# Expert rows gathered by index and expert results summed on chip by weighted selection products, in a three-block transformer kernel

## The chip, the core and the metric

The kernel runs on one NeuronCore of a Trainium2 chip. Its engines run side by side, each with its own instruction stream: TensorE (PE) multiplies matrices into PSUM, with a stream of its own for loading the stationary operand (PEld); VectorE (DVE), ScalarE (ACT) and GpSimd (POOL) work on rows in SBUF and PSUM; SyncE (SP) here only issues transfers. ACT and POOL issue transfers as well. Sixteen DMA engines carry them between HBM and SBUF. Engines wait for each other by semaphores. The metric is device time in microseconds, the median of several executions; everything is float32.

## What is computed

Three blocks act on 512 tokens of 1024 features: differential attention, latent attention (MLA), and a block of dilated attention beside a convolution, followed by a hierarchical mixture of experts. Each block scales and shifts its normed input by a modulation row, `silu(c) @ w + b`. The change touches the first modulation row and, above all, the mixture of experts:

```python
grp = argmax(hf @ w_rg + b_rg)                       # one of 4 groups
top_val, top_idx = lax.top_k(e_logits[grp], 2)       # two of its 8 experts
top_w = softmax(top_val) * p_grp
# every token goes to 2 of 32 experts; rows sorted by expert, padded
def expert_block(args):
    xblk, e = args
    return (silu(xblk @ w_gate[e]) * (xblk @ w_up[e])) @ w_down[e]
out = zeros((T + 1, D)).at[buf_tok].add(yb * buf_w[:, None])[:T]
y = x + gate * out ; result = rms_norm(y, g_final)
```

The three matrices of an expert are 1024x512, 1024x512 and 512x1024: 2 MB each, 6 MB an expert, 192 MB for all 32.

## The kernel before

**Expert stage.** `route` (on DVE) ranks the 32 experts by how many rows they have, and gives each rank a fixed number of row slots: 3 fixed experts with 64, 7 big ones with 128, 7 middle ones with 64, 15 small ones with 32 (`ROWS_OF`); rows beyond that would go to a loop of further items, which is skipped if none are left over. `Plan` makes 32 items in a fixed order: three fixed ones, then seven times (big, small, middle, small), then one small. An item has one or two pieces of at most 64 rows; there are 39 pieces (24 of 64 rows, 15 of 32).

**Rows in and out through HBM.** POOL writes zeros over the HBM buffer `expert_rows` (12.7 MB) and the end of `expert_results` early on (L1407), after routing scatters each of the 512 normed rows to its two slots (8 indirect transfers, L1423), and then loads each item's block of rows (`load_rows`, L1427). After an item ACT stores the gated results to `expert_results` (L1352). When all are stored, POOL gathers each token's two result rows (L1450) and DVE adds them with weights to `x` (`add_results`, L2082); a norm of each tile and the output store follow.

**One item on PE** (`item`, L992): `gate_up` (L979), transposes of the next item's rows (`flip_rows`, L950), transposes of the hidden rows (L1009), `down` (L989). A matrix product with 64-row pieces is made of pairs that write different halves of a PSUM bank's partitions, with 32-row pieces of fours. ACT does the silu and one PSUM copy, DVE the product (`swiglu`), the affine of the next rows (`flip`) and the gating of results (`gated_results`). The weights sit in three buffers; SP issues gate, up and down of item n+3 in order, each when item n has used its part (`load_expert`, L500).

**Records.** A float32 matmul of the program leaves two records in the trace: eight products of 512 columns for one token tile (`tokens`, L620) are 16 records. Transposes leave one.

**Head of the kernel.** DVE weighs and sums three units of the first modulation matrix (`weigh_unit`, 8 instructions each), and a fourth in halves (`weigh`), PE turns each sum into columns (`reduce_columns`), and from the columns comes the affine that the first projection waits for (L612, `unit[0] = MOD_RING` stands just before it). `scale_x` makes the normed rows, which PE transposes and ACT copies to `hT`.

Of the kernel before, what the change touches and what calls it, by code (L numbers as in the profile page):

```python
# [8 lines left out]
F32 = mybir.dt.float32  # L9
# [5 lines left out]
P = 128  # L15
T = 512
# [33 lines left out]
ZERO_P = 96  # L50
# [17 lines left out]
K_COLS = K_EXPERT + 1  # L68
# [70 lines left out]
def fused_kernel(nc, a, out, xs, ys):  # L139

    with ExitStack() as ctx:
# [45 lines left out]
        wts = sb("wts", [P, 2, TT])  # L187
# [56 lines left out]

        def c_loads():
            return [(silu_c[:, 8 * n:8 * n + 8], a[name][0].rearrange("(p k) -> p k", p=P)) for n, name in enumerate(("c", "c_2"))]
# [36 lines left out]
        mod_in = [sem(f"mod_half_loaded{i}") for i in range(2)]  # L283
        mod_used, mod_summed, mod_reduced = sem("mod_half_used"), sem("mod_unit_summed"), sem("mod_unit_reduced")
# [23 lines left out]
        zero_ready, zeros_out = sem("zero_ready"), sem("zeros_stored")  # L308
# [5 lines left out]
        rows_out = sem("rows_scattered")  # L314
# [10 lines left out]
        y_out = [sem(f"y_stored{n}") for n in range(5)]  # L325
        gath = [sem(f"results_gathered{t}") for t in range(TT)]
        out_done = sem("out_stored")
        xg_scaled = sem("rows_scaled")
        pe_passed, pool_passed = sem("pe_passed_waits"), sem("pool_passed_waits")
        prod_ready = sem("out_ready")  # L330
# [54 lines left out]
        y_at = [2 * D, 2 * D + W, 3 * D, 3 * D + W, 3 * D + W + 256]  # L385
        y_buf = [bufD[:, lo:lo + (256 if n > 2 else W)] for n, lo in enumerate(y_at)]
# [5 lines left out]

        h_act = [mix[:, 1, j * 256:(j + 1) * 256] for j in range(2)]
# [3 lines left out]
        class Piece:  # L397
# [3 lines left out]
            def __init__(self, bank, lo, size, used, buffer, stores):  # L401
                self.bank, self.lo, self.size, self.used = bank, lo, size, used
                self.buffer, self.stores, self.tiles = buffer, stores, P // size
                self.ff, self.cols = 2 * size * 2, 8 * size

        class Item:
# [4 lines left out]
            def __init__(self, n, p, q, rank, first, rows, pieces, loads, row_loads, free_bank, free_after):  # L411
                self.n, self.p, self.q, self.rank, self.first, self.rows, self.pieces = n, p, q, rank, first, rows, pieces
                self.loads, self.row_loads, self.free_bank, self.free_after = loads, row_loads, free_bank, free_after

        class Plan:


            def __init__(self):
                self.items, self.used, self.stores, self.loads, self.row_loads = [], [0, 0], [0] * 5, [0] * 3, [0, 0]
                self.last_piece, self.bank = [None] * 3, 1  # L420

            def add(self, rank):
                n, rows = len(self.items), ROWS_OF[rank]
                p, size = n % 3, min(rows, WIDE)
                pieces = []
                for lo in range(0, rows, size):
                    self.bank = 1 - self.bank
                    buffers = range(3) if size == WIDE else range(3, 5)
                    buffer = min(buffers, key=lambda m: self.stores[m])
                    pieces.append(Piece(self.bank, lo, size, self.used[self.bank], buffer, self.stores[buffer]))  # L430
                    self.used[self.bank] += 1
                    self.stores[buffer] += 1
                self.loads[p] += 1
                self.row_loads[n % 2] += n > 0
                before = self.last_piece[p]
                free_bank, free_after = (before.bank, before.used + 1) if before is not None else (0, 0)
                self.last_piece[p] = pieces[-1]
# [1729 lines left out]
```

## Time and profile before

| | |
|---|---|
| median of three runs | 1657.59 us (1657.05 to 1662.41) |
| the profiled execution's own time | 1660.52 us |
| its span in the trace | 1658.8 us |
| PE busy | 1414.1 us (85%) |
| DVE, ACT, POOL busy | 649.9, 357.7, 105.4 us |
| HBM read, written | 323.60 MB, 32.24 MB |
| expert stage (first `gate_up` to the last `down`) | 1114.6 to 1621.0 us |

All times are on the span's own clock, in microseconds from its start. The profile gives for each stretch how busy each engine was, the TensorE clock that was granted (1.00 is 2.4 GHz, 0.50 is 1.2 GHz), and the share of time in which the DMA engines had work. A chain of waits is followed back from the last instruction.

### The profile page before, as it was taken

The numbers are of one execution on the slowest core, as the hardware profiler recorded it, in microseconds if no ns is written. First come the engines' busy times: TensorE is split into PE (matmuls) and PEld (weight loads), VectorE is DVE, ScalarE is ACT, GpSimd is POOL, SyncE is SP. The second block draws the span as 40 slices with busy tenths as digits, with TensorE's granted clock in tenths as the row PEclk, the third lists the DMA queues.
The fourth block names the chain that finished last, engine by engine and source line by source line (L and its number), as shares of the span: only waits on it lengthen the run. The fifth ranks groups of instructions, "written<-read, shape, count | busy, mean of one in ns | idle before, by whom it ended". The sixth has DMA issues, their size and how long they took to land.

```text
span 1658.8 us, 16934 instructions
## 1 busy us (share of the span) xinstructions
PE 1414.1 (85%) x6444; PEld 720.2 (43%) x6444; DVE 649.9 (39%) x1178; ACT 357.7 (22%) x777; POOL 105.4 (6%) x236
## 2 busy tenths in 40 slices
PE   2899999889999999999799989959986877968770
PEld 2344443555455544664554456423433333323330
DVE  5675101995257422322589763242121111111113
ACT  2434101662211143441400063110000000000001
POOL 3000000010100000000200000120000000000005
PEclk9899999999999999999899989979997988989986
DMA  9663223920267523002424123159999999999994
GB/s 342 221 234 102 102 101 119 330 81 1 68 211 238 193 95 108 1 1 102 139 90 152 51 102 153 59 218 386 415 407 408 407 407 400 411 403 412 404 381 155
DMA packets 101337, 356.97 MB, mean 215 GB/s; under 512 B 9447, under 2 KB 15640, under 8 KB 92680
## 3 DMA queue, kind: packets, MB, share of 16 engines
q1 hardware_dynamic: 82512, 305.15, 48.5%
q0 software_dynamic: 9728, 34.47, 6.2%
q10 hardware_dynamic: 9016, 16.25, 2.7%
q8 instruction: 53, 0.87, 0.2%
q14 instruction: 28, 0.23, 0.0%
HBM read 323.60 MB, written 32.24 MB: 215 GB/s over the span
## 4 chain that ended last, share of the span: by engine, by line
PE 63%; DMA 17%; DVE 12%; ACT 3%; issue 2%; SPq 2%; POOL 1%; ACTq 0%; DVEq 0%; POOLq 0%
PE bank L620 15%; DMA slots<-in_w_exp_up 12%; PE score_banks L612 11%; PE score_banks L979 9%; PE score_banks L620 8%; DVE bufD L1945 5%; PE bank L989 4%; PE bank L596 4%; PE score_banks L768 2%; DMA slots<-in_w_exp_gate 2%; PE bank L832 2%; PE score_banks L825 2%; SPq L503 2%; DVE bufD L1606 1%; PE bank L772 1%
## 5 line engine op out<-in xcount | busy, mean ns | idle before, releaser
L620 PE MATMUL bank<-slots 128*128 128x512 f32 x608 | 265.1, 594 | 4.3 <-ACTq L1155 2.5
L612 PE MATMUL score_banks<-slots 128*128 128x512 f32 (+1 forms) x584 | 249.3, 586 | 15.1 <-ACTq L1081 6.2
L979 PE MATMUL score_banks<-slots,norm_row 128*64 128x512 f32 (+1 forms) x768 | 170.1, 618 | 54.5 <-DMA slots<-in_w_exp_up 42.3
L620 PEld LDWEIGHTS bank<-slots 128*128 128x128 f32 x608 | 114.0, 190 | 146.2 <-issue 142.9
L612 PEld LDWEIGHTS score_banks<-slots 128*128 128x128 f32 x584 | 114.3, 198 | 143.2 <-issue 129.5
L620 PE MATMUL score_banks<-slots 128*128 128x512 f32 (+1 forms) x384 | 157.3, 570 | 0.6 <-PE score_banks L620 0.3
L2045 DVE TENSOR_TENSOR mix<-probsT,score_banks 128x256 f32<-128x256 f32 (+1 forms) x39 | 14.4, 370 | 322.9 <-ACT probsT L1343 322.9
L979 PEld LDWEIGHTS score_banks<-slots,norm_row 128*64 128x64 f32 (+1 forms) x768 | 60.9, 145 | 157.9 <-issue 157.6
L989 PE MATMUL bank<-slots,mix 128*64 128x512 f32 (+1 forms) x864 | 116.9, 481 | 11.5 <-issue 10.4
L1343 ACT ACTIVATE probsT<-score_banks 128x256 f32<-128x256 f32 (+1 forms) x39 | 13.4, 343 | 463.5 <-PE score_banks L979 463.5
L620 PEld LDWEIGHTS score_banks<-slots 128*128 128x128 f32 x384 | 74.0, 199 | 78.2 <-issue 78.1
L979 PE MATMUL score_banks<-slots,mix 128*32 128x256 f32 (+1 forms) x960 | 79.4, 460 | 31.5 <-issue 28.9
L1945 DVE SCALAR_TENSOR_TENSOR bufD<-slots,col,bufD 128x512 f32<-128x512 f32 x120 | 80.5, 743 | 0.4
L1606 DVE SCALAR_TENSOR_TENSOR bufD<-slots,silu_c,bufD 128x512 f32<-128x512 f32 x98 | 73.7, 752 | 4.4 <-DMA slots<-in_w_mod 0.5
L989 PEld LDWEIGHTS bank<-slots,mix 128*64 128x64 f32 (+1 forms) x864 | 45.5, 122 | 67.3 <-issue 62.0
L979 PEld LDWEIGHTS score_banks<-slots,mix 128*32 128x32 f32 (+1 forms) x960 | 39.3, 130 | 75.7 <-issue 63.9
L1790 DVE TENSOR_REDUCE negmax<-score_banks 128x2 f32<-128x1024 f32 x32 | 39.0, 1221 | 63.4 <-PE score_banks L768 62.6
L1681 DVE TENSOR_TENSOR mix<-bank,gate_row 128x512 f32<-128x512 f32 x24 | 16.6, 691 | 118.4 <-PE bank L620 118.2
L1378 POOL TENSOR_SCALAR pw<-ss 128x1 f32<-128x1 f32 (+2 forms) x27 | 9.1, 339 | 766.9 <-ACT slots L1069 437.5
L1606 DVE SCALAR_TENSOR_TENSOR slots<-slots,silu_c 128x512 f32<-128x512 f32 x70 | 52.6, 751 | 12.9 <-DMA slots<-in_w_mod 7.9
L596 PE MATMUL bank<-k_sb,slots 128*128 128x128 f32 x312 | 48.6, 301 | 7.3 <-ACTq L1080 3.4
L596 PEld LDWEIGHTS bank<-k_sb,slots 128*128 128x128 f32 x312 | 37.4, 152 | 31.5 <-issue 19.5
(288 smaller groups left out, 1466.3 us busy)
## 6 DMA issues: line engine op xcount, KB each, us to landing
slots<-in_w_exp_down SPq DMA_DIRECT2D x32, 2048.0 KB, 36.3
slots<-in_w_exp_gate SPq DMA_DIRECT2D x32, 2048.0 KB, 30.9
slots<-in_w_exp_up SPq DMA_DIRECT2D x32, 2048.0 KB, 32.8
slots<-in_w_in SPq DMA_DIRECT2D x16, 2048.0 KB, 8.6
slots<-in_w_mod SPq DMA_DIRECT2D x24, 1024.0 KB, 5.1
slots<-in_ada_w SPq DMA_DIRECT2D x18, 1024.0 KB, 7.5
expert_rows<-norm_row POOLq DMA_DIRECT2D x1, 12672.0 KB, 50.4
slots<-in_w_out SPq DMA_DIRECT2D x6, 2048.0 KB, 7.9
```

What stands on the lines that cost most here:

```text
L503: sp.dma_start(dst, src).then_inc(e_in[it.p][j], 16)
L596: last = nc.tensor.transpose(bank[:, i * P:(i + 1) * P], piece, ident)
L612: last = mm(bank[:, cols], w[:, k, lo:lo + P], src[:, k, cols], start=(k == 0), stop=(k == kts - 1))
L620: last = mm(bank[:, 0:cols], src[:, k, t * P:(t + 1) * P], rhs(k), start=(k == 0), stop=(k == kts - 1))
L768: return mm(bank[:, :], A8[r, h, t * P:(t + 1) * P], B8[r, h, :], start=True, stop=True)
L825: mm(bank[:, :], hT[:, 2 * pair + c, t * P:(t + 1) * P], A8[:, 2 * pair + c, :], start=True, stop=False)
L832: last = mm(bank[:, c * P:(c + 1) * P], pT[:, j * P:(j + 1) * P], C_tok[:, j, h * P:(h + 1) * P], start=(j == 0), stop=(j == TT - 1))
L979: last = mm(out, rows[:, k, :], e_gu[it.p][:, :, k, c * pc.ff:(c + 1) * pc.ff], start=(k == 0), stop=(k == KT - 1))
L989: last = mm(psum[6 + pc.bank][c * pc.size:(c + 1) * pc.size, 0:pc.cols], hTe[pc.bank][:, lo:lo + pc.size], e_down[it.p][:, f, c * pc.cols: ...
L1606: return v.scalar_tensor_tensor(out=acc, in0=w, scalar=c, in1=acc, op0=ALU.mult, op1=ALU.add)
L1790: v.tensor_reduce(negmax[:, 2 * i:2 * i + 2], pair, AX.X, ALU.max, negate=True).then_inc(max_ready, 1)
L1945: conv_at[j] = steps(v.scalar_tensor_tensor(out=conv[:, j, :], in0=src, scalar=wcol, in1=conv[:, j, :], op0=ALU.mult, op1=ALU.add))
```

## The change

Four things are changed.

1. The normed rows are stored once to HBM, 512 rows (SP, before the last weight loads). A table of slots in HBM, 16 bytes a slot (token number, the number twice as float, weight), is filled with empty slots that name row 0 with weight 0; POOL scatters each token's 16 bytes to its two slots. ACT loads the slots back into SBUF before its first item, and POOL gathers each item's rows by these numbers.
2. Results are no longer stored. For each piece DVE makes two 128x256 matrices that hold a slot's weight where its token is (`selection`). Items form 17 groups of 1 to 3 pieces (`Plan.group`), and for each group PE multiplies, for each of 4 token tiles and 2 column halves, the selection with the results of every piece (`sum_up`: 64 rows contracted, 128 tokens by 512 columns) into one bank, and DVE adds the bank to `x` (`add_sum`). The 8 sums of a group are made during the items of the next group, in four places of each item; each sum first waits until DVE has taken the one before. The last group's sums follow at the end in four banks. The hidden rows' transposes of both piece kinds share one bank so that the other is free for the sums.
3. The final gain is loaded after the last item, and the end's norms are done for two tiles at a time.
4. At the head, unit 1 of the modulation is a row product on PE (`row_unit`) instead of eight DVE instructions, and PE runs 19 unused products before the first projection (`stay_warm`).

The routing weights are computed before the ranking instead of after it.

```diff
+            sp.wait_ge(xn_ready, 4 * TT)
+            sp.dma_start(xs.rearrange("(t p) d -> p t d", p=P), C_tok).then_inc(xs_out, 16)
             sp.wait_ge(logitsT_ready, 2)
             load_ahead(2, 1)
             sp.wait_ge(rows_picked, 1)
-            sp.wait_ge(rows_out, 16 * 2 * TT)
+            sp.wait_ge(xs_out, 16)
             load_ahead(2, 2)
...
+            def row_unit():
+                pe.wait_ge(silu_ready, 1)
+                pe.wait_ge(w_in[1], unit_arrival(1))
+                bank = tr_banks.claim(pe)
+                for k in range(KT):
+                    last = mm(bank[0:1, :], silu_c[:, k:k + 1], unit_view(1)[:, k, :], start=(k == 0), stop=(k == KT - 1))
...
+            def stay_warm(n):
+                for _ in range(n):
+                    mm(psum[5][:, 0:P], ident, ones, start=True, stop=True)
...
             reduce_columns()
-            reduce_columns()
+            row_unit()
...
+            def sum_up(pieces, j, bank, done):
+                t, half = j % SUMS // 2, j % 2
+                r = slice(half * WIDE, (half + 1) * WIDE)
+                for pc in pieces:
+                    last = mm(bank[:, :], pc.select[t // 2][r, t % 2 * P:(t % 2 + 1) * P], y_buf[pc.buffer][r, :],
+                              start=pc is pieces[0], stop=pc is pieces[-1])
+                last.then_inc(done, 1)
+
+            def sums(js):
+                for j in js:
+                    g = j // SUMS
+                    if j % SUMS == 0:
+                        pe.wait_ge(select_ready, made_until[g])
+                        for pc in plan.groups[g]:
+                            pe.wait_ge(y_ready[pc.bank], pc.used + 1)
+                    if j > 0:
+                        pe.wait_ge(sum_taken, j)
+                    sum_up(plan.groups[g], j, psum[5], summed_up)
+
             def item(it, ahead=None, unrolled=True):
-
+                after_gate_up, after_flip, after_h, after_down = sums_of(it) if unrolled else [()] * 4
...
+                sums(after_gate_up)
                 for pc in it.pieces:
-                    if ahead is not None and pc is it.pieces[-1]:
-                        flip_rows(ahead)
+                    if pc is it.pieces[-1]:
+                        if ahead is not None:
+                            flip_rows(ahead)
+                        sums(after_flip)
...
+                sums(after_h)
                 pe.wait_ge(e_in[it.p][2], 16 * it.loads)
...
+                sums(after_down)
...
-                for pc in it.pieces:
-                    act.wait_ge(y_ready[pc.bank], pc.used + 1)
-                    for c in range(pc.tiles):
-                        act.dma_start(ys[bass.ds(it.first + pc.lo, pc.size), c * pc.cols:(c + 1) * pc.cols],
...
-                    gp.indirect_dma_start(xs[:, :], bass.IndirectOffsetOnAxis(ap=dest[:, k, t:t + 1], axis=0),
-                                          C_tok[:, t, :], None).then_inc(rows_out, 16)
-            pool.wait_ge(rows_out, 16 * 2 * TT)
+                    gp.indirect_dma_start(table[:, :], bass.IndirectOffsetOnAxis(ap=dest[:, k, t:t + 1], axis=0),
+                                          own_slot[:, k * TT + t, :], None).then_inc(slots_out, 16)
...
-                gp.dma_start(xg[it.q][0:it.rows], xs[bass.ds(it.first, it.rows), :]).then_inc(xg_in[it.q], 16)
+                gp.indirect_dma_start(xg[it.q][0:it.rows], None, xs[:, :],
+                                      bass.IndirectOffsetOnAxis(ap=it.row_ids[0:it.rows, 0:1].bitcast(I32), axis=0)).then_inc(xg_in[it.q], 16)
...
+            def selection(pc, ready):
+                for h in range(2):
+                    v.tensor_scalar(pc.select[h], tokens_256, pc.slots[:, 1 + h:2 + h], pc.slots[:, 3:4], ALU.is_equal, ALU.mult)\
+                        .then_inc(ready, 1)
+
+            def add_sum(j, bank, done, taken, n):
+                t, cols = place_of_sum(j)
+                dve.wait_ge(done, n + 1)
+                v.tensor_tensor(x[:, t, cols], bank[:, :], x[:, t, cols], ALU.add).then_inc(taken, 1)
...
             weigh_unit(0)
-            weigh_unit(1)
+            dve.sem_inc(unit_used, 1)
             scale_x(0)
```

## Rows read from the trace of the kernel before

**Rows 1.** The page: busy time and share of PE.

```profile
PE 1414.1 (85%) x6444; PEld 720.2 (43%) x6444; DVE 649.9 (39%) x1178; ACT 357.7 (22%) x777; POOL 105.4 (6%) x236
```

**Rows 2.** Stretches of the expert stage: us; busy us by engine; clock, DMA share, GB/s.

```profile
1243.60:1309.60 66.00, 51.88 (x372) 23.08 (x368) 10.34 (x22) 3.40 (x10) 2.07 (x4) 0.87 1.02 407
...
1514.30:1576.10 61.80, 47.06 (x331) 20.33 (x328) 8.31 (x17) 2.94 (x9) 1.51 (x3) 0.89 1.02 407
```

**Rows 3.** Chain of waits, expert stage: start us, us, what it went through.

```profile
1157.67 13.73 PE score_banks L979 x64
...
1514.24 33.73 DMA slots<-in_w_exp_up
1548.06 15.54 PE score_banks L979 x64
```

**Rows 4.** PE's instructions in order of time, about one round of four items.

```profile
1242.42 7.09 PE L979 MATMUL score_banks<-slots,norm_row 128*64 128x512 f32 x32 [3.63 <-issue]
...
1251.47 3.65 PE L989 MATMUL bank<-slots,mix 128*64 128x512 f32 x16 [0.52 <-issue]
...
1293.22 0.44 PE L1009 MATMUL bank<-k_sb,mix 128*128 128x128 f32 x2
...
1301.97 3.66 PE L979 MATMUL score_banks<-slots,mix 128*32 128x256 f32 x64
...
1309.70 5.80 PE L979 MATMUL score_banks<-slots,norm_row 128*64 128x512 f32 x26 [0.44 <-issue]
```

**Rows 5.** Chain of waits: three token tiles of a projection, the router's products.

```profile
739.00 20.60 PE bank L620 x48
...
1078.70 7.04 PE score_banks L918 x32
```

**Rows 6.** Records of two lines: duration ns min/median/max, times, contracted rows by columns.

```profile
L825 PE MATMUL score_banks<-slots x64: 592/592/697, 644.5 to 726.0; 128*128 128x512 f32 x64
L828 PEld LDWEIGHTS score_banks<-slots x64: 182/184/186, 646.4 to 726.7; 64*128 64x128 f32 x64
L828 PE MATMUL score_banks<-slots x64: 589/641/693, 646.4 to 727.1; 64*128 64x512 f32 x64
```

**Rows 7.** DVE, one result's addition to `x` in the block's projection.

```profile
1046.84 0.69 DVE L1684 TENSOR_TENSOR x<-x,mix 128x512 f32<-128x512 f32 x1
```

**Rows 8.** Transfers by line: KB each, median us to landing.

```profile
expert_results<-bufD ACTq DMA_DIRECT2D x48, 128.0 KB, 7.6
...
expert_results<-bufD ACTq DMA_DIRECT2D x60, 32.0 KB, 6.3
```

**Rows 9.** All engines in order of time, routing to the second item.

```profile
1101.44 1.23 POOL L1423 DMA_INDIRECT expert_rows<-slots,dest  x1 [18.78 <-DVEq L1553]
...
1106.29 0.16 DVE L1579 TENSOR_TENSOR wts<-bufD 128x4 f32<-128x4 f32 x1
...
1125.37 1.06 PE L950 MATMUL score_banks<-k_sb,bufD 64*128 64x64 f32 x8 [2.11 <-DMA bufD<-expert_rows]
```

**Rows 10.** All engines in order of time, the head.

```profile
22.41 5.47 DVE L1606 SCALAR_TENSOR_TENSOR bufD<-slots,silu_c,bufD 128x512 f32<-128x512 f32 x7
22.51 0.71 POOL L1388 TENSOR_TENSOR ss<-pw 128x4 f32<-128x4 f32 x1
...
31.17 0.60 DVE L1605 TENSOR_SCALAR bufD<-slots,silu_c 128x512 f32<-128x512 f32 x1 [0.23 <-DVEq L1642]
...
49.75 29.25 PE L612 MATMUL score_banks<-slots 128*128 128x512 f32 x64 [3.64 <-ACTq L1177]
```

**Rows 11.** All engines in order of time, the end.

```profile
1611.75 5.80 PE L979 MATMUL score_banks<-slots,norm_row 128*32 128x256 f32 x64 [6.87 <-issue]
...
1619.08 1.93 PE L989 MATMUL bank<-slots,mix 128*32 128x256 f32 x32 [0.41 <-issue]
...
1649.04 1.06 ACT L1364 ACTIVATE slots<-x 128x1024 f32<-128x1024 f32 x1 [3.29 <-DVEq L2088]
...
1652.95 1.28 DVE L2092 SCALAR_TENSOR_TENSOR slots<-x,ss,gate_row 128x1024 f32<-128x1024 f32 x1 [1.81 <-POOL ss L1388]
```

More of the change, by code:

```diff
@@ L415, in fused_kernel @@
         class Plan:
             def __init__(self):
-                self.items, self.used, self.stores, self.loads, self.row_loads = [], [0, 0], [0] * 5, [0] * 3, [0, 0]
+                self.items, self.groups = [], []
+                self.used, self.loads, self.row_loads = [0, 0], [0] * 3, [0, 0]
                 self.last_piece, self.bank = [None] * 3, 1
[L422 to L437, printed above, removed]
-                self.items.append(Item(n, p, n % 2, rank, FIRST_ROW[rank], rows, pieces, self.loads[p], self.row_loads[n % 2],
-                                       free_bank, free_after))
@@ new lines, in group @@
+            def group(self, *ranks):
+                wides = [0, 1] if len(self.groups) % 2 == 0 else [2]
+                narrow, found = 3 + len(self.groups) % 2, []
+                for rank in ranks:
+                    n, rows = len(self.items), ROWS_OF[rank]
+                    p, size = n % 3, min(rows, WIDE)
+                    pieces = []
+                    for lo in range(0, rows, size):
+                        self.bank = 1 - self.bank
+                        at_row = FIRST_ROW[rank] + lo
+                        slots = wide_slots[:, at_row // WIDE] if size == WIDE else narrow_slots[:, (at_row - WIDE_ROWS) // NARROW]
+                        pieces.append(Piece(self.bank, lo, size, self.used[self.bank], wides.pop(0) if size == WIDE else narrow,
+                                            slots, select[len(found) + len(pieces)]))
+                        self.used[self.bank] += 1
+                    found += pieces
+                    row_ids = big_slots[:, rank - FIXED] if rows > WIDE else pieces[0].slots
+                    self.loads[p] += 1
+                    self.row_loads[n % 2] += n > 0
+                    before = self.last_piece[p]
+                    free_bank, free_after = (before.bank, before.used + 1) if before is not None else (0, 0)
+                    self.last_piece[p] = pieces[-1]
+                    self.items.append(Item(n, p, n % 2, rank, rows, row_ids, pieces, self.loads[p], self.row_loads[n % 2],
+                                           free_bank, free_after))
+                self.groups.append(found)
@@ L1167, in _ @@
             table_column(col1, R1_ROWS)
+            bank = tr_banks.take(act)
+            fn(mod_acc(1)[0:1, :], bank[0:1, :], ACT.Copy).then_inc(tr_freed, 1)
+            act.wait_ge(tr_freed, tr_banks.n)
+            act.sem_inc(row_copied, 1)
             for k in range(KT):
@@ new lines, in item @@
+            def item(it, after):
+                after_gate_up, after_flip, after_h, after_down = sums_of(it)
+                swiglu(it)
+                add_sums(after_gate_up)
+                add_sums(after_flip)
+                if after is not None:
+                    flip(after, it)
+                add_sums(after_h)
+                gated_results(it)
+                add_sums(after_down)
+                for g in plan.groups:
+                    if it.pieces[-1] is g[-1]:
+                        if g is plan.groups[0]:
+                            dve.wait_ge(first_slots_in, 16)
+                            dve.wait_ge(slots_in, 16 * (3 + P // NARROW))
+                        for pc in g:
+                            selection(pc, select_ready)
```

313 lines of the change are left out of this document (209 added, 104 removed).

## The prediction

> **What bounds the kernel now.** I read the page first: PE is busy for 85% of the span [rows 1], so most stages hang on PE. The one stage where PE has room is the expert stage, and it is there that the change puts work on PE. The stretches of that stage [rows 2] show the DMA engines with work all the time (share 1.02) at 407 GB/s while PE is busy for 51.9 of 66.0 us and 47.1 of 61.8 us, at a granted clock of 0.87 and 0.89: part of the time at 1.2 GHz instead of 2.4. The chain of waits [rows 3] says the same: a big item's `gate_up`, then 33.7 us of an up matrix on its way, then the next big item. So weights coming in set the pace: from the first big item at 1157.67 to the last item at 1611.75 it is seven rounds of four items in 454.1 us, 64.9 a round [rows 3, 11].
>
> What PE itself needs for a round comes from its instructions in order of time [rows 4]. Big: 13.73 of `gate_up` at full clock [rows 3], then 1293.22 to 1301.97 = 8.75 for transposes and `down`. Small: 1301.97 to 1309.70 = 7.73. Middle: 1242.42 to 1251.47 + 3.65 = 12.70. Small again 7.73. Together 13.73 + 8.75 + 7.73 + 12.70 + 7.73 = 50.6 us. PE has some 14 us of room a round. The question is how this compares with what the sums need.
>
> **The price of one sum.** A sum's product streams 512 columns over 64 contracted rows into 128 outputs. Three token tiles of a projection, 24 products of 512 columns over 128 rows, take 20.60 us [rows 5]: 0.86 each. No row shows a lone product of 512 columns over 64 rows, so the price is bounded: below by half, 0.43, if 64 rows cost half of 128; above by 0.86 plus two weight loads of 0.184 laid open, 1.23 [rows 6]. I take 0.86. Two rows are nearest. The records of 64 contracted rows last no less than those of 128, 589 against 592 ns at the least, 641 against 592 in the median [rows 6]. And the router's 16 products, 8 of 384 columns and 8 of 128 with only 36 outputs, take 7.04 us [rows 5]; by columns alone they would take 8 x 0.64 + 8 x 0.215 = 6.9. A quarter of the array used costs what the whole costs. That `gate_up` and `down` are cheaper per product is no counterexample: their pairs and fours write different partitions and run side by side. The sums don't: the pieces of one sum read the same 64 rows and add to one bank, and the next sum, on the other 64 rows, waits for `sum_taken`.
>
> The Trainium skill says the same of this against the change: by "TensorE: Matmul & The Clock Gate" (the table of what to do, small-K matmuls) a single K=32 matmul takes the time of K=128 and the gain is in tiles that run concurrently. Its "TensorEngine Tiling (Array Packing)" (theoretical speedup) promises up to 2x for a dimension of 64, which would be the 0.43 if the halves overlapped; the semaphore between them forbids it here. The same page (key properties) says that a change of tiling mode drains the engine; the records show no more than a fraction of a microsecond at such a change, and by either reading the forecast stays.
>
> **Sum over the expert stage, part by part.**
> *Head of the stage.* The ranking comes 6 small DVE instructions of 0.16 to 0.18 later (`wts` was made at 1106.29 [rows 9], off the path; now it is before the ranks), plus three for the slot words: +1.1 us to `pick_rows` and the first item. The 8 scatters stay on POOL (1.23 each [rows 9]) and move 16 bytes instead of 4 KB a row. Behind them ACT now waits with its first silu, and issues 8 loads of slots; POOL's first gather waits for the first of these. The nearest row is the rows of item 1, which PE waited 2.1 us for [rows 9]: I keep that wait and allow -2 to +6. The big weights are loaded earlier by some 6 us, which is worth nothing if PE is the bound. Filling 32 KB instead of 17 MB with zeros lay beside attention and is worth nothing on the path either.
> *Group 0* (2 pieces) is summed within item 2, two sums in each of four places: 16 products x 0.86 = 13.8. The second sum of each place waits for DVE: an addition takes 0.69 [rows 7] and I put 0.2 on it for two semaphores, so 4 x 0.9 = 3.6. For entering and leaving a sum I take 0.1 (bounds 0 and 0.4, the idle time put down to "issue" where a product follows another engine's copy [rows 4]): 8 x 0.1 = 0.8. Together 18.2.
> *Seven rounds.* The groups of a round have 3 and 2 pieces, 8 sums each: (3 + 2) x 8 = 40 products x 0.86 = 34.4; 16 entries x 0.1 = 1.6; one sum per place, so DVE's addition is hidden by a flip, a `gate_up` or a `down`; only between the sum after the flip and the one after the hidden transposes does PE wait some 0.5, and that takes the place of the 0.4 to 0.5 that it waited for ACT's copy [rows 4]. A round is 50.6 + 34.4 + 1.6 = 86.6; seven are 606.2, less 8 x 0.86 = 6.9 because the first round sums a group of one piece: 599.3.
> *DMA in a round*: stores of results go, 48 x 128 KB + 60 x 32 KB = 8.3 MB [rows 8], 20.4 us in the stage at 405 GB/s, 2.6 a round, so DMA needs about 64 of 86.6: hidden now. Rows gathered by index are as many bytes as before; empty slots read row 0. Requested two items ahead, they have over 20 us: nothing, unless a gather took three times the plain load's time. DVE gets 16 additions and 10 selections of at most 0.4 more a round, 15 us, and has had 10 busy of 66 [rows 2].
> *Last item.* It needs 1611.75 + 3.6 to 1621.0, at full clock 6.3 [rows 11]; the sums of the group before it, 2 pieces, 2 per place, add 13.8 + 0.8 + 3.6 and 0.5 at the transposes: 25.0.
>
> **The end.** Before, from the last `down` at 1621.01 to 1658.8: 37.8 us of stores, gathers, additions, norms and output [rows 11]. After: addition and two selections 1.5; 8 products 6.9 in four banks, PE the slower of the two; last addition 0.8; square and rstd of the last tiles as in 1649.04 to 1652.95, 3.9; two last norms of 1.28, 2.6; the last store and the end as from 1654.23 on, 4.6. Sum 20.3: a gain of 17.5, but only after the last item.
>
> **The head of the kernel.** Now DVE weighs unit 1 until 27.88, then scales x, and starts unit 2 at 31.17 [rows 10]. After, DVE scales x once POOL's rstd is there, 22.51 + 0.71 = 23.2; the 3.3 from 27.88 to 31.17 then end at 26.5, if unit 2 has landed (the third of three 2 MB units; I allow until 27.5). So 4 earlier, and the 19 unused products spare part of the slow start at 49.75, where 32 products take 29.25 instead of 32 x 0.86 = 27.5 [rows 10]: 1 of 1.7. PE's row product is 8 x 0.86 = 6.9 from 21.9, or twice that at half clock, and the transposes and ACT's copies queue behind it on PE: at worst the gain is 1. Bounds 0 and 7; I take 5. It is carried whole, since the following stages are PE's.
>
> **Total.** 1157.7 - 5.0 + 1.1 + 18.2 = 1172.0; + 599.3 = 1771.3; + 25.0 = 1796.3; + 20.3 = 1816.6 us of span. The profiled execution is 1.7 over its span and 2.9 over the median: 1816.6 + 1.7 - 2.9 = 1815.4 us, 9.5% slower. In all 312 products x 0.86 = 268 us come to PE, and it had some 14 us a round free.
>
> **Rivals.**
> *Half price* (64 rows cost half, 0.43): round 50.6 + 17.2 + 1.6 = 69.4, group 0 11.3, last item 18.1, end 19.0: 1165.1 + 482.4 + 18.1 + 19.0 - 1.2 = 1683 us. For it speaks only that two 64-row products in different row halves follow each other closely; against it the records' length. Chance 0.07.
> *Faster*: the sums vanish in PE's waiting and DMA, freed of 8.3 MB, sets the end. This decides below 0.86 - (1815.4 - 1657.6) / 312 = 0.35 us a product. Last item's start 1611.75 - 20.4 - 1 = 1590.4, plus 12 and 18: 1619 us. It needs consecutive sums to overlap in the array, which the wait for `sum_taken` speaks against. Chance 0.04.
> *Open weight loads*: each product pays its two loads of 0.184 as well, because products in one row half can't load behind each other: 312 x 0.37 = 115 more, 1930 us. Against it: 8 transposes of 64 rows take 1.06 us, 0.13 each, though all read the same rows and each has a load of its own [rows 9]. Chance 0.09.
> That the sums don't do what they say would need the overflow loop, which did not run before; nothing changes that.
>
> **How the numbers follow.** The forecast has 0.80. Its own ends: entries at 0 and DVE waits at nothing, head 7, -22, 1793, and another 20 if the base round has slack that the sums fill (the 0.4 to 0.6 waits, 7 x 2.5): 1773. Upwards: entries at 0.3 (+26), head 0 (+5), slots +6, and DVE late by 0.1 at each of 136 sums (+14): 1866. The range 1770 to 1868 leaves out the three rivals, 0.20. What a measurement can tell from no change is about 0.3%: faster 0.04, same 0.01, slower 0.95.
>
> **What would show it.** In the profile after: `sum_up` x624 records (312 products) with a pace of 0.86 us; the DMA share in the rounds falling from 1.02 to about 0.75; PE clock 1.00 and PE busy over 95%; big items 86 to 87 us apart; 37.8 us after the last `down` turned to about 24 after it; `win0`'s first product at about 45. The prediction is wrong if a product of 64 rows is paced at 0.5 or less, or if PE still waits for an up matrix in the later rounds.

## The result

The changed kernel takes 1958.43 us (median of 4 runs, 1949.13 to 1959.71) against 1659.66 us for the kernel before on the same chip: ratio 1.1793, 95% interval 1.1769 to 1.1817. So it is 17.9% slower, where 9.5% was forecast, and its time lies outside the range given. The profiled execution took 1959.71 us with a span of 1957.9 us. The direction and what bounds the new kernel were forecast rightly; the price was forecast at about half of what it is. Of the executions reported below one, of `split`, took 1662.73 us at a lower granted clock (0.956) than its other four (0.963 to 0.966) and is left out of its ratio.

The page of the changed kernel: PE is busy for 93% of the span (85% before, [rows 1]). The second line is TensorE's granted clock in 40 slices, in tenths of full speed.

```profile
PE 1821.4 (93%) x7122; PEld 842.8 (43%) x7122; DVE 755.9 (39%) x1384; ACT 357.0 (18%) x778; POOL 98.9 (5%) x217
...
PEclk9999999999989999999899779888978787888876
```

Stretches of the expert stage, three of the seven rounds of four items (the columns are those of [rows 2]: us; busy us by engine; clock, DMA share, GB/s):

```profile
1182.00:1275.00 93.00, 91.06 (x450) 34.08 (x448) 24.99 (x49) 3.41 (x10) 3.58 (x4) 0.88 0.74 278
...
1477.60:1582.00 104.40, 102.11 (x459) 38.66 (x460) 25.00 (x48) 3.41 (x10) 3.57 (x4) 0.84 0.68 254
1582.00:1689.00 107.00, 105.32 (x458) 39.17 (x460) 25.00 (x48) 3.41 (x10) 3.57 (x4) 0.81 0.66 243
```

The DMA engines, at 1.02 in [rows 2], now have work for 0.66 to 0.74 of the time (until the last weights are in), and PE is busy for 98% of it. So the bound did move from the weights' transfers to PE, as forecast. But a round was to last 86.6 us, the first one 79.7, and they last 92 (the first) to 107. The last but one column says why: PE is busy and yet was granted only 0.81 to 0.88 of its clock. The product of one minus the clock and the stretch, summed over the seven rounds, is some 118 us (clocks of 0.88, 0.85, 0.85, 0.84, 0.81, 0.82 and 0.81), and the seven rounds took 720.1 us where 599.3 were forecast, 120.8 more.

PE's instructions in order of time, a place where the clock falls (the answer to [rows 4]: start us, us, line, tiles, shape, records):

```profile
1491.44 1.12 PE L1079 MATMUL bank<-bufD,probsT 64*128 64x512 f32 x2
1492.40 1.02 PE L1079 MATMUL bank<-gate_row,slots 64*128 64x512 f32 x2
1493.35 0.44 PE L1115 MATMUL bank<-k_sb,mix 128*128 128x128 f32 x2
1493.72 1.06 PE L1031 MATMUL score_banks<-k_sb,bufD 32*128 32x32 f32 x8
1494.71 1.12 PE L1079 MATMUL bank<-bufD,probsT 64*128 64x512 f32 x2
1495.67 1.02 PE L1079 MATMUL bank<-gate_row,slots 64*128 64x512 f32 x2
...
1497.89 2.07 PE L1079 MATMUL bank<-bufD,probsT 64*128 64x512 f32 x2 [0.84 <-DVE x L2227]
1499.76 1.91 PE L1079 MATMUL bank<-gate_row,slots 64*128 64x512 f32 x2
1501.60 8.58 PE L1070 MATMUL bank<-slots,mix 128*64 128x512 f32 x32
```

The first two sums go at 0.96 and 0.95 us a product: the 0.86 of the forecast and some 0.1 at either end of a sum. The third sum, 64 rows again, takes twice that, and the `down` behind it 8.58 us where it takes 7.09 at full clock (a line of `rows128` below). That is the level of 1.2 GHz in place of 2.4, granted between one sum and the next while PE had had work all the time but for 0.84 us. In this round it happens four times, for 6 to 14 us each. Three of these stretches, with two at full clock between them (PE alone, then the clock, DMA share, GB/s):

```profile
1497.60:1503.60 6.00, 5.71 (x10) 0.52 1.00 381
1503.60:1521.60 18.00, 17.38 (x114) 0.97 0.62 226
1521.60:1528.60 7.00, 7.00 (x37) 0.51 0.98 418
1528.60:1541.60 13.00, 13.00 (x52) 1.00 0.70 245
1541.60:1555.60 14.00, 13.77 (x24) 0.52 0.59 236
```

The last of these falls comes with no wait ahead of it: the second of three products already takes longer, the third twice its time.

```profile
1541.02 1.12 PE L1079 MATMUL bank<-bufD,probsT 64*128 64x512 f32 x2
1541.99 1.69 PE L1079 MATMUL bank<-bufD,slots 64*128 64x512 f32 x2
1543.47 1.91 PE L1079 MATMUL bank<-bufD,gate_row 64*128 64x512 f32 x2
```

Each fall comes within or just ahead of the second or third sum of the group of places around the short transposes, where PE had streamed through 32 or 64 rows for some microseconds, apart from 0.33 to 0.44 us of transposes over 128. The clock comes back within the `down` over 128 rows that follows, or just behind it. This reading is a guess until something but the rows is held fixed, which is what the first experiments do.

### The profile page after: what moved, and what is told of

Read it like the earlier page. It is cut to its first block, busy times and chain, and to the rows that moved or that the text cites. A ratio compares the mean times of both kernels' runs of the same rounds, so it can differ in the third digit from the quotient of the medians.

```text
span 1957.9 us, 18533 instructions
## 1 busy us (share of the span) xinstructions
PE 1821.4 (93%) x7122; PEld 842.8 (43%) x7122; DVE 755.9 (39%) x1384; ACT 357.0 (18%) x778; POOL 98.9 (5%) x217
## 4 chain that ended last, share of the span: by engine, by line
PE 82%; DVE 11%; DMA 3%; ACT 2%; issue 2%; POOL 1%; DVEq 0%; SPq 0%; ACTq 0%; POOLq 0%
PE bank L1079 19%; PE bank L679 13%; PE score_banks L1060 11%; PE score_banks L671 9%; PE bank L1070 8%; PE score_banks L679 7%; DVE bufD L2104 4%; PE bank L655 3%; PE score_banks L1031 2%; DVE x L2227 2%; PE bank L913 1%; PE score_banks L849 1%; PE score_banks L906 1%; DMA slots<-in_ada_w 1%; PE bank L853 1%
## 5 line engine op out<-in xcount | busy, mean ns | idle before, releaser
L2227 DVE TENSOR_TENSOR x<-bank,x 128x512 f32<-128x512 f32 x128 | 88.5, 691 | 306.4 <-PE bank L1079 306.4
L1079 PE MATMUL bank<-bufD,probsT 64*128 64x512 f32 x256 | 172.2, 758 | 21.3 <-DVE x L2227 21.2
L1070 PE MATMUL bank<-slots,mix 128*64 128x512 f32 (+1 forms) x864 | 163.3, 657 | 1.1 <-ACT mix L1476 1.1
L1060 PE MATMUL score_banks<-slots,norm_row 128*64 128x512 f32 (+1 forms) x768 | 161.8, 588 | 0.0
L1060 PEld LDWEIGHTS score_banks<-slots,norm_row 128*64 128x64 f32 (+1 forms) x768 | 52.6, 137 | 108.4 <-issue 107.2
L1079 PE MATMUL bank<-bufD,slots 64*128 64x512 f32 x128 | 82.2, 728 | 0.0
L1079 PEld LDWEIGHTS bank<-bufD,probsT 64*128 64x128 f32 x256 | 43.1, 210 | 83.1 <-DVE x L2227 41.9
L1079 PE MATMUL bank<-bufD,gate_row 64*128 64x512 f32 x112 | 76.1, 768 | 0.0
L1079 PE MATMUL bank<-gate_row,slots 64*128 64x512 f32 x112 | 74.8, 756 | 0.0
L1060 PE MATMUL score_banks<-slots,mix 128*32 128x256 f32 (+1 forms) x960 | 67.1, 399 | 1.7 <-DVE mix L2197 1.7
```

The source lines that it names most:

```text
L1060: last = mm(out, rows[:, k, :], e_gu[it.p][:, :, k, c * pc.ff:(c + 1) * pc.ff], start=(k == 0), stop=(k == KT - 1))
L1070: last = mm(psum[6 + pc.bank][c * pc.size:(c + 1) * pc.size, 0:pc.cols], hTe[pc.bank][:, lo:lo + pc.size], e_down[it.p][:, f, c * pc.cols: ...
L1079: last = mm(bank[:, :], pc.select[t // 2][r, t % 2 * P:(t % 2 + 1) * P], y_buf[pc.buffer][r, :], start=pc is pieces[0], stop=pc is pieces[-1])
L2227: v.tensor_tensor(x[:, t, cols], bank[:, :], x[:, t, cols], ALU.add).then_inc(taken, 1)
```

## The experiments

In the short diffs, lines with + are the experiment's and lines with - the changed kernel's (for the kernels that start from the kernel before, this is said). The kernel before was measured beside each group of runs: 1658.97 us beside `rows128`, `rows96`, `one_piece` and `bf16`; 1662.01 beside `head_only`, `stored`, `split` and `rows128_mode`; 1661.58 beside `half128` and `no_warm`. Ratios are against the one of the same group. `rows128`, `rows96`, `rows128_mode`, `half128` and `one_piece` were each executed once; the others 5 to 12 times.

### The same products over 128 and over 96 rows

```diff
-                r = slice(half * WIDE, (half + 1) * WIDE)
+                r = slice(0, 2 * WIDE)
```

> The changed kernel with one edit: every sum's product contracts all 128 rows instead of 64 (the results are not the reference's, since both column halves are added). Columns streamed, waits and places are the same. Theory A, the granted clock falls because products over 64 rows count as too little work for TensorE: granted clock at least 0.97 in the seven rounds, a round 87 to 89 us instead of 102 to 107, total about 1835. Theory B, the clock falls because each sum is a short burst between waits and transposes, whatever its rows: clock 0.81 to 0.88 as in the changed kernel, total about 1958. Theory C, the sums are slow by a change of tile mode or a bank shared with VectorE, not by the clock: the pace stays at 1.9 us for two products where the clock is full, total above 1900.

Measured: 1826.13 us, span 1824.3, clock 0.974 over the span. Theory A held; B and C fall. As many products, as many columns, as many waits; only the contracted rows are 128. A round, and the same stretch with 96 rows (`r = slice(0, 96)`), of each kernel one line:

```profile
1336.33:1424.08 87.75, 84.99 (x458) 34.72 (x460) 25.01 (x48) 3.42 (x10) 3.57 (x4) 1.00 0.80 300
```

```profile
1335.04:1422.79 87.75, 85.00 (x458) 34.77 (x460) 25.01 (x48) 3.41 (x10) 3.58 (x4) 1.00 0.80 299
```

In `rows128` the sum behind a wait for DVE, and the `down` that follows it, at the place of the first fall above:

```profile
1356.11 1.12 PE L1079 MATMUL bank<-bufD,probsT 128*128 128x512 f32 x2 [0.64 <-DVE x L2227]
1357.07 1.02 PE L1079 MATMUL bank<-gate_row,slots 128*128 128x512 f32 x2
1358.02 7.09 PE L1070 MATMUL bank<-slots,mix 128*64 128x512 f32 x32
```

> As with 128 rows, but 96 rows contracted for both halves (again not the reference's results). Theory A: the fall gets smaller with the rows, so a clock between 0.85 and 1.00 and a total between 1835 and 1958; the run shows whether 96 rows are enough. Theory B: 0.81 to 0.88 and about 1958.

Measured for 96 rows: 1824.73 us, clock 0.976. The pace within a sum is the same 0.96 and 0.95 us as with 64 rows. So of the 132 us between the changed kernel and `rows128` some 130 come from the low clock, and the low clock comes with the products' 64 rows. (The rest is no effect of the sums: the router's products start 3.3 us earlier in this execution of `rows128`, and up to them the two kernels are the same.) 96 rows do as well as 128. The records say the same in their durations (ns, min/median/max), first those of the changed kernel, then those of `rows128`:

```profile
L1079 PE MATMUL bank<-bufD,gate_row x112: 588/590/1058, 1231.6 to 1900.2; 64*128 64x512 f32 x112
```

```profile
L1079 PE MATMUL bank<-bufD,gate_row x112: 592/592/593, 1215.3 to 1775.3; 128*128 128x512 f32 x112
```

### Is it the rows, or the change between kinds of products?

`rows128`, and before each sum one product over 64 rows and only 32 columns, whose place the sum then overwrites:

```diff
+                low = slice(half * WIDE, (half + 1) * WIDE)
+                mm(bank[:, 0:32], pieces[0].select[t // 2][low, t % 2 * P:(t % 2 + 1) * P], y_buf[pieces[0].buffer][low, 0:32], start=True, stop=True)
```

> The kernel whose sums contract 128 rows (its sums are therefore not the reference's), and before each sum one more product over 64 rows and only 32 columns, into a place that the sum then overwrites: 128 of these in a run of the seven rounds and the last item. It keeps the changes between products over 64 and over 128 rows and leaves out nearly all columns streamed through 64 rows. Theory A (the granted clock falls with the columns that are streamed through half of the rows): clock 0.97 or more, rounds 88 to 90 us, about 1835 us. Theory B (the changes themselves bring the clock down): clock 0.81 to 0.90 and rounds of 100 us and more, about 1940 us.

Measured: 1879.26 us, span 1877.4, clock 0.971. A round:

```profile
1356.70:1449.70 93.00, 90.25 (x491) 39.40 (x490) 25.00 (x48) 3.42 (x10) 3.57 (x4) 1.00 0.76 283
```

The clock stays at 1.00 in six of the seven rounds (0.98 in the first) with 16 more products over 64 rows a round, so the changes between 64 and 128 rows do not bring it down. But the total missed: 93.0 us a round where 88 to 90 were expected. The added product takes 0.33 us from start to start for 32 columns, 16 x 0.33 = 5.3 a round. I had priced it by its columns. All 136 added products make 45 of the 53 us over `rows128`; the other 8.1 stand before the router's products, where the two kernels are the same. A float32 product is two records, each with a load of its weights that lasts 0.185 us in the mean here. That these loads are laid open with so few columns is my reading; no run tests it.

### Half of the sums over 64 rows

```diff
+                r = slice(0, 2 * WIDE) if half == 0 else slice(WIDE, 2 * WIDE)
```

> Half of the sums contract 128 rows, those of the first 512 columns of a token tile, and half contract 64 as in the change (the sums over 128 rows are therefore not the reference's). Nothing else differs. Theory (each product over 64 rows brings the granted clock down a little, and the loss goes by their number): half of the 120.8 us that the seven rounds took over the forecast, so clock about 0.91 and rounds of some 96 us, total about 1890 us. Rival (one kind of product decides whole: with some at 128 rows between them the clock stays up, or it falls all the same): 1830 us with clock 1.00, or 1950 us with clock 0.84.

Measured: 1864.31 us, clock 0.952. Three of its rounds:

```profile
1345.70:1433.40 87.70, 85.54 (x459) 34.48 (x458) 25.00 (x48) 3.42 (x10) 3.58 (x4) 1.00 0.80 300
1433.40:1525.70 92.30, 90.04 (x459) 35.78 (x458) 25.00 (x48) 3.41 (x10) 3.57 (x4) 0.94 0.76 284
1525.70:1617.70 92.00, 90.09 (x459) 35.85 (x458) 24.98 (x48) 3.42 (x10) 3.57 (x4) 0.94 0.76 286
```

Both expectations missed. The loss is not in proportion to the number of such products: two rounds show none (87.6 and 87.7 us) and five lose 1.5 to 4.6 us against `rows128`, where half of the loss would be some 8. Nor does one kind decide whole. With the same instructions a round can keep the clock or lose it, so what the clock does in a round can't be told from its instructions alone here. It stays open what sets it off.

### One piece for each sum

The sums take the first piece of their group only, so 136 products are left (`for pc in pieces[:1]`), all over 64 rows; the other pieces' results are left out.

> The changed kernel with only the first piece of a group in each sum (the others are left out): 136 products instead of 312, the same number of sums, waits and additions. 176 products fewer at 0.86 us and full clock are 151 us. Theory A: 64-row work is a smaller share, the clock is at least 0.95, a round about 50.6 + 13.8 + 1.6 + 2 = 68 us, total 1680 to 1705. Theory B: the bursts and waits are as many, clock about 0.85, a round about 78, total about 1765.

Measured: 1723.94 us, clock 0.941, between the two expectations. Its rounds last 70.8 to 74.5 us at a clock of 0.91 to 0.95, with the DMA share at 0.92 to 0.95 in the five between the first and the last. At full clock PE's work would be 50.6 + 16 x (0.86 + 0.2) = 67.6 us. 16 products over 64 rows a round lose 3 to 7 us here, in every round, where the 20 among 20 full ones of `half128` lost 0 to 4.6.

### Cheaper products

`bf16`: the selection holds zeros and ones in bfloat16, the weight is applied in float32 where the results are written, and the results are rounded to bfloat16. The products keep their 64 rows.

```diff
+                    sel = pc.select[t // 2].bitcast(BF16)
+                    last = mm(bank[:, :], sel[r, t % 2 * P:(t % 2 + 1) * P], y_buf[pc.buffer].bitcast(BF16)[r, 0:W],
...
+                    v.scalar_tensor_tensor(out=y_buf[pc.buffer].bitcast(BF16)[:, 0:W].rearrange("p (c n) -> p c n", c=times),
```

> The changed kernel with the selection as zeros and ones in bfloat16, the results rounded to bfloat16 and multiplied by the slot's weight while they are gated: the same 312 products at a quarter of the passes, about 0.22 us each. Price theory (what a product streams is all that counts): PE needs 50.6 + 40 x 0.22 + 2 = 61 to 63 us a round, the weights need 64 at 407 GB/s, so DMA sets the round again: 64 to 66 us, total 1625 to 1650, faster than before. If the clock falls with these products too (0.85 or less), a round is 68 to 72 and the total 1660 to 1700.

Measured: 1642.07 us (5 runs, 1639.38 to 1649.25), ratio 0.9906, interval 0.9875 to 0.9936: 0.9% faster than the kernel before, as the price theory had it. The DMA share is back at 1.01. The clock is mostly up, but not always: between 0.89 and 0.99 in the stretches of the rounds, which last 61.2 to 67.6 us. A round:

```profile
1300.00:1364.00 64.00, 60.94 (x428) 24.10 (x427) 25.67 (x53) 3.85 (x12) 4.44 (x5) 0.99 1.01 406
```

`split` keeps about twice the digits of `bf16`, though not all of float32's (how near its output comes to float32 is not told here): each weighted result is written as its bfloat16 rounding and as the remainder, again in bfloat16, one in each half of the 128 rows, and one bfloat16 product over 128 rows adds both.

```diff
-                    last = mm(bank[:, :], pc.select[t // 2][r, t % 2 * P:(t % 2 + 1) * P], y_buf[pc.buffer][r, :],
+                    last = mm(bank[:, :], pc.select[t // 2][:, t % 2 * P:(t % 2 + 1) * P], y_halves(pc)[half],
...
+                    own = (slice(0, WIDE), slice(WIDE, P))
+                    for h, y in enumerate(y_halves(pc)):
+                        v.tensor_copy(y[own[h], :], y_whole[own[h], :]).then_inc(y_step, 1)
+                    dve.wait_ge(y_step, done + 3)
+                    for h, y in enumerate(y_halves(pc)):
+                        v.tensor_tensor(y[own[1 - h], :], y_whole[own[h], :], y[own[h], :], ALU.subtract)\
```

> The change with its sums kept at near float32 accuracy, but built otherwise: each piece's gated results (weighted in float32) are written as two bfloat16 numbers, the rounded value and what is left, in the two halves of the 128 rows, and one bfloat16 product over 128 rows with a selection of zeros and ones takes both at once. Theory (the price of a product in float32, and the clock that 64 rows bring, are all that went wrong): as the bfloat16 run, rounds of 64 to 65 us set by the transfers with DMA share about 1.0, granted clock at least 0.95 in them, 1640 us, between 1632 and 1650. Rival (VectorE's five instructions for a piece in place of one, with three waits between them, hold up the next group's products): rounds of 66 us or more and 1650 to 1670 us.

Measured: 1640.05 us, ratio 0.9865, interval 0.9851 to 0.9879. It has the lowest time of all, though its interval overlaps that of `bf16`. The first theory held in the total, and its rounds are even shorter than expected: three of 61.0 to 61.3 us, then four of 63.0 to 63.6. Two stretches, the clock higher than in `bf16` or equal:

```profile
1283.30:1344.30 61.00, 57.86 (x417) 23.44 (x416) 35.11 (x69) 3.41 (x10) 3.58 (x4) 1.00 1.01 400
...
1469.30:1533.30 64.00, 59.45 (x416) 24.87 (x416) 34.20 (x66) 3.41 (x10) 3.58 (x4) 0.97 1.01 410
```

Against `rows128` with its 87.75 us, a round with its 40 products costs at least 26.75 us less in bfloat16, 0.67 a product; within a sum they now follow each other after 0.23 us. DVE's extra work shows (35 us busy in place of 25), but PE waits for none of it in these rounds: what it waits for on DVE are the additions, as before, 0.7 us at most each time.

### The other parts of the change alone

`head_only` is the kernel before with `row_unit` and `stay_warm`; `no_warm` is the same without the 19 unused products.

> The kernel before with one part of the change alone: modulation unit 1 as a row on TensorE with ScalarE's copy and the two runs of small products (6 and 13) that stand around it. Everything from the routing on is as before. Theory (the head's gain is on the path and is carried whole): the first product of the window part stands about 5 us earlier, and every later mark with it, since the rounds of the experts take what the DMA takes: 1654 us, ratio 0.9969. Rival (a wait for a transfer later on takes it back): the router's marks come earlier and the end doesn't, 1659 us, ratio 1.000.

> The head's row unit alone, without the 6 and the 13 small products that stand around its reduction; all else as before. In the trace of before the eight small products ahead of the first projection took 1.86 us and its first 25 records 12.51 us, against 1.05 and 10.9 with the small products. Theory (the row unit brings the first projection forward, and the small products give another 2.4 us through the clock): first projection's product at about 46.0, and 1.6 us more for its first records; 1654.3 us where the kernel with the small products took 1651.9, ratio 0.9955. Rival (the small products are the whole gain, because the row's own chain is no shorter): first product at 49 or later, 1659 us, ratio 0.999.

Measured: `head_only` 1651.9 us, ratio 0.9942, interval 0.993 to 0.9954; `no_warm` 1657.27 us, ratio 0.9971, interval 0.9959 to 0.9984. Both rivals fall: the head's gain reaches the end, and the row unit has a gain of its own. It is larger than I expected for `head_only` (9.6 us in place of 5.1) and smaller for `no_warm`. The first projection's products, `head_only` and then `no_warm` (in the kernel before they start at 49.75 [rows 10]):

```profile
45.19 17.00 PE L617 MATMUL score_banks<-slots 128*128 128x512 f32 x39 [0.64 <-ACTq L1208]
```

```profile
45.28 17.11 PE L617 MATMUL score_banks<-slots 128*128 128x512 f32 x33 [3.65 <-ACTq L1206]
```

Both start 4.5 us earlier than before. With the unused products ahead PE then makes 39 records in 17.0 us, without them 33 in 17.11: 15 us at a granted clock of 1.00 against 0.81, 2.8 us. Before, the slow start cost 1.7 us [rows 10]. So 4.5 + 1.7 = 6.2 of the 9.6 us have their place; in the profiled executions `head_only` is 6.6 us ahead at the first big item (1151.03 against 1157.67 in [rows 3]) and 3.3 at the end. The rest lies within what executions of these kernels differ by (1649.38 to 1657.22), and I have no row for it. How large this scatter is shows at the router's products: eight profiled kernels here (the changed one and its variants but `stored`) have the same code up to there, and start them between 1069.25 and 1078.39 us, 1072.9 in the mean.

`stored` is the change without its sums: rows gathered by index, the new head, and the results stored and fetched as before.

> The change without its sums: the experts' rows are gathered by index from the normed rows, the head has the row unit, but the weighted results are stored to HBM by row and fetched back per token as before. Theory (what made the change slow lies in the sums alone, and the index gather costs little): the rounds are set by the transfers as before, some 67 us at 407 GB/s; head -5.0, the routing +1.1 with the last of the first loads issued up to 8 us earlier: 1648 us, between 1643 and 1655, ratio 0.993, granted clock over 0.9. Rival (the gather by index on GpSimd is itself late and holds up the rounds): rounds over 70 us and over 1670 us.

Measured: 1652.87 us, ratio 0.995, interval 0.9938 to 0.9962. It can't be told from `head_only`. The gather by index costs nothing and brings nothing that can be measured; the whole loss is in the sums.

## Why the prediction was wrong in size and right in kind

**The step that failed** is "PE clock 1.00" in the list of what would show it, and with it every term of the sum that priced PE's work at full clock. I read the clock of 0.87 and 0.89 in [rows 2] as that of an engine which waits for weights, and took for granted that an engine without waits is granted 2.4 GHz. The runs showed a clock of 0.81 to 0.88 in rounds in which PE is busy for 98% of the time, and 16 us a round lost by it. None of the rows showed a stretch of PE full of 64-row products, so nothing bore that out, and it should have been bounded: at the lower level for the whole of the sums' 34.4 us a round it would have been 34 us more. With the clock held up by 96 or 128 rows, the forecast's own span of 1816.6 us is met within 0.5% (1822.9 and 1824.3). Its terms against both kernels, in us:

| term | forecast | `rows128` | changed kernel |
|---|---|---|---|
| first big item starts | 1172.0 | 1167.7 | 1180.7 |
| seven rounds | 599.3 | 608.1 | 720.1 |
| last item with its sums | 25.0 | 26.3 | 36.1 |
| the end | 20.3 | 22.1 | 21.1 |
| span | 1816.6 | 1824.3 | 1957.9 |

Of the 141.3 us by which the changed kernel's span is over the forecast, 133.6 are the difference to `rows128`, nearly all of it the clock; 7.7 are errors of mine, on balance. Of the 133.6, 3.3 stand before the router's products and have nothing to do with the sums. The 7.7 are what is left of +8.8 in the rounds, +1.3, +1.8 and a start that was 4.3 us earlier than forecast, by an amount in which executions of the same code differ. That the span fits so well is in part luck.

**A product of 64 rows costs 0.86 us: right.** Within sums of three pieces the starts at full clock are 0.96, 0.86 and 0.95 us apart. *Half price* and *open weight loads* are both refuted, the latter although its 1930 us came nearest to the measured time: at full clock a product follows the one before it within a sum after 0.86 us, where laid-open loads would have made it 1.23. A total alone would have confirmed the wrong rival.

**0.1 for entering and leaving a sum: too little.** It is 0.2 (0.96 + 0.95 for two products of 0.86). 16 x 0.1 = 1.6 more a round; `rows128` has 87.75 for the forecast's 86.6.

**DVE's additions hidden in the rounds, 0.9 laid open where two sums follow each other: right.** In the last item PE waits 0.85 each time for the bank:

```profile
1908.78 1.91 PE L1079 MATMUL bank<-gate_row,slots 64*128 64x512 f32 x2
1911.54 2.07 PE L1079 MATMUL bank<-bufD,probsT 64*128 64x512 f32 x2 [0.85 <-DVE x L2227]
```

The lines also show the clock: 1.9 us a product, twice what it takes at full clock. From 1900.80 to 1936.90 the clock was 0.67, and the last item took 36.1 us for 25.0; at full clock it is 26.3. Of those 1.3 us over the forecast, 0.8 are the eight entries at 0.2 in place of 0.1, and the 6.3 us for the item alone were too few: its rows give 3.6 and, from 1617.55 to 1621.0, 3.5 [rows 11].

**Group 0, 18.2 us: right in its terms, wrong in the clock.** From item 2's `gate_up` (the third item) to the first big item it was 12.5 us before; `rows128` takes 31.2 (+18.7) and the changed kernel 41.4 (+28.9) at a clock of 0.70.

**The head, 5.0 us: right way, perhaps too small.** The router's products start at 1073.55 for 1078.70 in [rows 5], 5.15 earlier; over the eight executions named above it is 0.3 to 9.5, 5.8 in the mean, so the 5.15 of this one is no close proof. By the medians of `head_only` the head brings 9.6 us, of which 6.2 have their place. DVE waited for unit 2 until 27.52, as allowed. Of the 1.7 us of slow start I had counted 1 as saved; with the clock at 1.00 all of it goes.

**The routing, +1.1: about right.** From the router's products to the second item's `gate_up` it took 54.01 us before and 53.26 in the changed kernel, 0.75 less. But this is no fair pair, since scatters and clock differ between executions. The kernels with the old routing and the new head took 50.50 (`head_only`) and 52.45 (`no_warm`). `stored`, with the new routing and `down` at full clock as in `head_only`, took 51.84, which is 1.3 more; the changed kernel, with its `down` at the lower clock as in `no_warm` (5.35 us for 3.65), took 0.8 more. The steps ahead of the scatter cost 0.7 of it, as I said of them. Scatter, load of the slots and first gather in the changed kernel:

```profile
1106.40 5.53 DMA expert_slots<-sums,dest
1111.95 2.08 DMA w_router<-expert_slots
...
1114.86 4.46 DMA bufD<-normed_rows,w_router
```

**DMA about 0.75, hidden: right** (0.66 to 0.74, lower because the rounds are longer, and 0.37 in the last round, when the weights run out; 0.80 in `rows128`). A down matrix now lands in 8.0 us where it queued for 36.3.

**The end, 20.3: right** (21.1). **Faster below 0.35 us a product: right in kind, not in its 1619 us.** The bfloat16 products lie below it (0.23), and both kernels with them are faster than before. In `split` the last item starts at 1597.9 for the rival's 1590.4, takes 17.7 us for 12, and the end 23.2 for 18. The rounds are not held by the DMA engines all the way: in the three of 61 us PE waits for nothing but DVE's additions, and only in the later ones does it sit idle ahead of a `gate_up`, three times for 5.9 us together, at a DMA share of 1.01. Nor is the gain that of the stores' 20.4 us in the stage. Against the trace of `head_only`, which has the same head, the last item starts 9.2 us earlier (4.2 of them stand before the router's products and are the scatter of executions), takes 8.5 longer for its sums, and the end is 16.1 shorter. So most of it comes from the end, where no result is stored and gathered any more.

The prediction weighed two rules. The Trainium skill, "TensorE: Matmul & The Clock Gate" (small-K matmuls), says that a single product over 32 rows takes as long as one over 128. The runs agree, for 64 and 96 rows: 0.86 us at full clock with each. The Trainium skill, "TensorEngine Tiling (Array Packing)" (key properties), says that a change of tiling mode drains the engine. A tenth of a microsecond may be just that. Most neighbours of the sums, `gate_up` and `down`, fill 64 or 32 outputs and so differ in shape from the sums of both kernels, and there the last product takes 0.95 us in both. But ahead of the hidden rows' transposes, which use 128 rows and 128 outputs, it takes 0.95 us over 64 rows (1492.40 to 1493.35, in the first listing) and 0.85 over 128, here in `rows128`, and 0.85 over 96 too:

```profile
1351.11 1.02 PE L1079 MATMUL bank<-gate_row,slots 128*128 128x512 f32 x2
1351.96 0.38 PE L1115 MATMUL bank<-k_sb,mix 128*128 128x128 f32 x2
```

The 0.33 us of the tiny product in `rows128_mode` might hold a drain as well; that run doesn't tell it from the weight loads.

## What to carry to other kernels

Work that is put into an engine's free time is paid for in full once that time is used up: compare its price with the room first (here 34.4 us of products for 14 us of room), and make the product cheaper before it is moved there. A forecast that makes TensorE the bound must bound the granted clock too, above all where the new float32 products use half of the rows; if the operands can be laid out over 96 or 128 rows at no cost in instructions, that is worth trying (here it was 130 us). Where the total fits a rival, look for its mechanism in the records before believing it. And two marks in one execution each tell a gain of some microseconds only if executions of the same code agree at that mark.

## What was not expected of the hardware

Float32 products that contract 64 rows let the granted clock fall to its lower level again and again (0.81 to 0.88 in the mean of a round) in an engine that is busy for 98% of the time; over 96 or 128 rows the clock is 1.00 with the same products and the same pace. The loss does not go by their number: 40 a round lose 16 us, 20 among 20 full ones up to 4.6 or none, 16 alone 3 to 7. Whether the rows themselves are the cause, or something that goes with them, was not measured. Products over 96 rows are like those over 128 also in the 0.85 us ahead of the transposes, so it is not told apart whether the count of rows matters or only that it is no more than half of them; and the variants over 96 and 128 rows multiply more data besides. No run had the same data, spread with zeros over 128 rows.
